# A one-core fp32 block pair kernel: the second in-projection as five Strassen pairs, with its inputs, trig tables and residual copies placed around the pooling blocks

## The reference

```python
h = x @ w_in                       # 1024 x 2368
x_q, x_kv, k_rope_raw, gate_a, u_pool, gate_b = jnp.split(h, splits, axis=-1)   # 512 256 64 512 512 512
y_a = mla_branch(x_q, x_kv, k_rope_raw, positions, ...) * jax.nn.silu(gate_a)
y_b = pool_branch(u_pool, pool_w, pool_scale) * jax.nn.silu(gate_b)   # window means of 2, 4, 8, 16, minus u; one 128x128 product per group
x = layer_norm(alpha * x + concatenate([y_a, y_b]) @ w_out, ln_g, ln_b)
```

## Time and profile before

| | us |
|---|---|
| median of 3 runs (lowest, highest) | 1684.1 (1683.61, 1685.53) |
| the profiled execution's own time | 1683.6 |
| its span, first to last instruction | 1681.8 |
| PE busy in the span | 1666.5 |
| mean granted TensorE clock | 0.997 |

### The profile page before, as it was taken

One profiled execution on the slowest core, in us unless ns is written; L12 is line 12 of the kernel. 1 busy time (PEld: TensorE's weight loads), 2 busy tenths in 40 slices (PEclk: granted clock), 3 DMA queues, 4 the chain that ended last, 5 costly groups with the idle time before them and its releaser, 6 DMA issues.

```text
span 1681.8 us, 20879 instructions
## 1 busy us (share of the span) xinstructions
PE 1666.5 (99%) x7597; PEld 1373.9 (82%) x7597; DVE 1256.2 (75%) x1494; ACT 795.6 (47%) x1066; POOL 452.0 (27%) x270
## 2 busy tenths in 40 slices
PE   9999999999999999999999999999999999999998
PEld 7788788888787888888888888888888888788786
DVE  6478791369999888888888879889737936777654
ACT  5667741236854433444344444455332327566531
POOL 4223222100015654555454000005432442201000
PEclk9999999999999999999999999999999999999999
DMA  7111112053412232222322974762322221010351
GB/s 265 52 48 37 50 51 76 25 213 94 169 51 88 76 98 75 75 87 84 91 75 96 327 267 153 247 195 62 101 88 63 88 88 31 26 63 26 114 218 75
DMA packets 161098, 176.99 MB, mean 105 GB/s; under 512 B 13566, under 2 KB 114692, under 8 KB 161028
## 3 DMA queue, kind: packets, MB, share of 16 engines
q1 hardware_dynamic: 158708, 167.67, 30.7%
q10 hardware_dynamic: 2320, 8.39, 1.3%
HBM read 140.38 MB, written 35.65 MB: 105 GB/s over the span
## 4 chain that ended last, share of the span: by engine, by line
PE 93%; DVE 4%; ACT 1%; issue 1%; DMA 1%; DVEq 0%; SPq 0%; ACTq 0%
PE ps L962 31%; PE ps L2603 27%; PE ps L2557 19%; PE ps L2849 5%; PE ps L2834 3%; PE ps L2499 1%; PE ps L2685 1%; PE ps L2888 1%; PE ps L2806 1%; DVE pt_lo L2376 1%; PE ps L2523 1%; DVE prob L2333 1%; PE ps L2822 1%; DMA x_tok<-in_x 1%; ACT pt_hi L1646 0%
## 5 line engine op out<-in xcount | busy, mean ns | idle before, releaser
L985 POOL TENSOR_TENSOR w_lo<-w_raw,w_hi 128x1024 fp32r<-128x1024 f32 x52 | 138.0, 2654 | 594.1 <-ACT w_hi L1097 592.3
L2603 PE MATMUL ps<-hop_hi_P,wop_hi_P 128*128 128x512 f32 x672 | 263.6, 392 | 2.0 <-DVE u L1974 0.8
L2603 PE MATMUL ps<-hop_lo_P,wop_hi_P 128*128 128x512 f32 x672 | 262.9, 391 | 0.0
L2603 PE MATMUL ps<-hop_hi_P,wop_lo_P 128*128 128x512 f32 x672 | 262.8, 391 | 0.0
L991 POOL TENSOR_TENSOR wop_lo_P<-pair_sum,wop_hi_P 128x512 fp32r<-128x512 f32 x90 | 137.3, 1526 | 351.5 <-ACT wop_hi_P L1108 351.5
L962 PE MATMUL ps<-h_hi,w_hi 128*128 128x512 f32 x688 | 214.1, 392 | 0.0
L962 PE MATMUL ps<-h_lo,w_hi 128*128 128x512 f32 x688 | 211.9, 389 | 0.0
L962 PE MATMUL ps<-h_hi,w_lo 128*128 128x512 f32 x688 | 211.8, 389 | 0.0
L962 PEld LDWEIGHTS ps<-h_hi,w_hi 128*128 128x128 f32 x688 | 128.2, 188 | 30.0 <-issue 4.3
L2603 PEld LDWEIGHTS ps<-hop_hi_P,wop_hi_P 128*128 128x128 f32 x672 | 126.9, 189 | 30.5 <-DVE u L1974 1.6
L962 PEld LDWEIGHTS ps<-h_lo,w_hi 128*128 128x128 f32 x688 | 129.1, 188 | 27.1
(11 more groups left out here) (386 smaller groups left out, 3403.8 us busy)
## 6 DMA issues: line engine op xcount, KB each, us to landing
pair_raw<-in_w_up SPq DMA_DIRECT2D x48, 512.0 KB, 4.9
w_raw<-in_w_in SPq DMA_DIRECT2D x46, 512.0 KB, 3.9
dn_raw<-gu_park SPq DMA_DIRECT2D x84, 256.0 KB, 3.9
dn_raw<-in_w_down SPq DMA_DIRECT2D x60, 256.0 KB, 3.1
gu_park<-up_cv SPq DMA_DIRECT2D x24, 512.0 KB, 2.6
out_raw<-in_w_out SPq DMA_DIRECT2D x30, 256.0 KB, 2.8
x_tok<-in_x SPq DMA_DIRECT2D x4, 1024.0 KB, 8.1
x_park<-xs SPq DMA_DIRECT2D x1, 4096.0 KB, 13.2
```

What stands on the lines that cost most here:

```text
L985: nc.gpsimd.tensor_tensor(lo[:, :], raw[:, :], hi[:, :].bitcast(f32), ALU.subtract).then_inc(w_lo_done, 1)
L2603: mm = nc.tensor.matmul(dst, w[q][:, k, :], x[q][:, k, :], start=a, stop=b, skip_group_check=True)
```

## The change

Of the 19 blocks only the 8 for pooling and the rope key stay blocks, and they come first (the head blocks are now u and gate_b of group 0). The 10 others (6 latents, 4 gates) become five Strassen pairs after them: kv; q 0 and 1; q 2 and 3; gates 0 and 1; gates 2 and 3. The PE stream and what it waits for:

```diff
-            for i in range(2, Q_TILES + KV_TILES):
...
-            pe.wait_ge(ga_done, 3)
-            project(N_KR, 0, ps[0], h_hi, h_lo)
+            block_with(N_POOL + 2, ps[0], lambda: (pe.wait_ge(final_gain, 16), pe.wait_ge(gb_done, 1), by_token(0)))
+            by_token(1)
+            pe.wait_ge(rstd3_spread, 1)
+            block_with(N_POOL + 3, ps[1], lambda: (by_token(2), pool_product(0)))
+            by_token(3)
...
+            block_with(N_KR, ps[0], lambda: pool_product(3))
...
+        IN_RUN = ("P1", "P6", "P5", "P2", "P7")
+        IN_ORDER = [(q, 0) for q in IN_RUN]
+        for n in range(IN_PAIRS - 1):
+            IN_ORDER += [("P1", n + 1), ("P4", n), ("P3", n)] + [(q, n + 1) for q in IN_RUN[1:]]
+        IN_ORDER += [("P4", IN_PAIRS - 1), ("P3", IN_PAIRS - 1)]
...
+                if q == "P1":
+                    pe.wait_ge(*((yb_done, 4), (kr_scaled, 1), (lat_done, 2), (lat_done, 4), (lat_done, 6))[n])
+                elif q == "P6":
+                    pe.wait_ge(*((tok_copied, NT), (gb_done, 4), (lat_done, 1), (lat_done, 3), (lat_done, 5))[n])
+                    if n in (2, 4):
+                        pe.wait_ge(root2_done, n // 2)
+                elif q == "P2":
+                    pe.wait_ge(s1c_done, PAIRS + n + 1)
+                else:
+                    need = {"P7": "U2", "P4": "U3", "P3": "C22"}.get(q)
+                    if need:
+                        pe.wait_ge(sums_done, in_sums(need, n))
+                pe.wait_ge(wop_lo_done, in_made(q, n))
...
+            for q, n in IN_ORDER:
+                in_product(q, n)
+                if (q, n) == ("P1", 2):
+                    pe.wait_ge(acc_kv_done, KV_TILES)
+                    spread_mean_squares(acc_kv, 0)
+                elif (q, n) == ("P2", 3):
+                    pe.wait_ge(acc_q_done, Q_TILES)
+                    pe.wait_ge(lat_done, Q_TILES + KV_TILES)
+                    spread_mean_squares(acc_q, 1)
...
                 if j == 0:
+                    pe.wait_ge(ga_done, 1)
+                elif j == 1:
                     pe.wait_ge(ga_done, 4)
...
+                elif j == 3:
+                    pe.wait_ge(ga_done, 2)
```

The order of the pairs (n = 0 to 4), first on DVE, then on ACT:

```diff
+            for n in range(IN_PAIRS):
+                in_third_sums(n)
+                if n == 2:
+                    latent_factor(0, T2)
+                elif n == 3:
+                    latent_factor(1, T1)
+                    latent_factor(1, T2)
+                    latent_normed(0)
+                    latent_normed(1)
+                elif n == 4:
+                    latent_low(2)
+                    gate2(1)
+                    gate2(0)
+                in_result(n, 1)
+                if n == 4:
+                    gate2(3)
+                in_result(n, 0)
+                if n + 1 < IN_PAIRS:
+                    in_second_sum(n + 1)
+                if n == 1:
+                    latent_factor(0, T1)
+                elif n == 2:
+                    latent_normed(4)
+                    latent_normed(5)
+                elif n == 3:
+                    latent_normed(2)
+                    latent_normed(3)
+                    latent_low(0)
+                if n + 2 < IN_PAIRS:
+                    in_weight_sums(n + 2)
+            gate2(2)
...
+            for n in range(-1, IN_PAIRS):
+                last = n + 1 == IN_PAIRS
+                if not last:
+                    in_high("P7", n + 1)
+                    in_first_sum(n + 1)
+                if n == 1:
+                    latent_root(0)
+                if not last:
+                    in_high("P4", n + 1)
+                if n == 3:
+                    latent_high(0)
+                    latent_high(1)
+                if 0 <= n < 3:
+                    latent_square(PAIR_LATS[n][1])
+                elif n >= 3:
+                    gate_tanh2(2 * n - 5)
+                if not last:
+                    in_high("P3", n + 1)
+                if n == 4:
+                    park_gate(3)
+                if 0 <= n < 3:
+                    latent_square(PAIR_LATS[n][0])
+                elif n >= 3:
+                    gate_tanh2(2 * n - 6)
+                for q in IN_NEXT:
+                    if n + 2 < IN_PAIRS:
+                        in_high(q, n + 2)
+                if n == 2:
+                    latent_root(1)
+                if n == 3:
+                    latent_high(2)
+                    latent_high(3)
+                    act.wait_ge(wop_lo_done, in_made("P3", IN_PAIRS - 1))
+                    high(N_UQ)
+                    park_gate(1)
+                    park_gate(0)
+                elif n == 4:
+                    park_gate(2)
+            act.wait_ge(product, in_run("P5", IN_PAIRS - 1))
+            act.wait_ge(latn_done, Q_TILES + KV_TILES)
+            high(N_UQ + 1)
+            act.wait_ge(pos_in, POS_BACK)
+            act.wait_ge(sums_done, in_sums("C12", IN_PAIRS - 1))
+            swap_halves(0, kr_raw)
```

The weights of a pair have one buffer, loaded in two halves on SP:

```diff
+            for n in range(IN_PAIRS):
+                if n == 0:
+                    sp.wait_ge(block_done, N_KR)
+                for f in range(2):
+                    if n >= 1:
+                        sp.wait_ge(pair_sum_done, 4 * PAIRS + 4 * n)
+                        sp.wait_ge(wop_lo_done, in_made(("P2", "P4")[f], n - 1))
+                    sp.dma_start(in_raw[f][:, :, :], w2_v[:, :, IN_COLS[n][f]:IN_COLS[n][f] + P]).then_inc(pair_in[f], 16)
+            sp.wait_ge(wop_lo_done, in_made("P3", IN_PAIRS - 1))
+            sp.wait_ge(product, in_run("P5", IN_PAIRS - 1))
 ...
```

More of the change, by code:

```diff
@@ L846, in _, with nope_load @@
             load(n, 0, *[(dst[:, :, h, :], uq[:, :, h, NOPE:QK]) for h in range(HEADS)])
-            for b in range(2):
+            def nope_load(b):
                 n = N_UQ + 1 + b
@@ L1066, in _ @@
+            pool.wait_ge(gate_parked[1], GATE + 16)
+            low(N_UQ + 1)
+            low(N_UQ + 2)
+            latent_low(5)
+            for n in range(N_UQ + 3, N_BLOCKS):
+                low(n)
             pool.wait_ge(block_done, N_BLOCKS - 1)
@@ L1535, in _ @@
[L1535 to L1549 removed]
+                act.dma_start(res_park[t], tok_out[t % 2][:, :]).then_inc(res_parked[t % 2], 16)
@@ L1576, in _, with park_pooled @@
-            gate(0)
-            park_pooled(3)
-            gate(1)
-            gate(2)
-            gate(3)
-            for q in range(2):
-                act.wait_ge(gate_parked[q], GATE + 16 * HEADS // 2)
+                    act.wait_ge(y_parked, 16 * (g - 1))
+                nc.scalar.activation(y_pool[:, g % 2, :], ps[3 if g == 0 else 1][:, :], ACT.Tanh, scale=0.5).then_inc(th_done, 1)
+            def park_pooled(g):
+                act.wait_ge(yb_done, g + 1)
+                act.dma_start(y_park[4 + g], y_pool[:, g % 2, :]).then_inc(y_parked, 16)
@@ new lines, in _ @@
+            pooled_gate(1)
+            pool_gate(2, "P6")
+            mix_sum("P4")
+            mix_low("P7")
+            mix_low("P6")
+            pooled(3)
+            pool_weight(3)
+            pooled_gate(2)
+            pool_gate(3)
+            in_weight_sums(0)
+            pooled_gate(3)
+            mix_low("P4")
+            for parked in res_parked:
+                dve.wait_ge(parked, 16 * NT // 2)
+            dve.wait_ge(block_done, read(N_KR))
+            V.tensor_tensor(kr_out[:, :], ps[0][:, :], rstd3[:, :], ALU.mult).then_inc(kr_scaled, 1)
@@ L2723, in _, with pool_product, block_with @@
-            pe.wait_ge(lat_done, 5)
-            project(N_POOL, 0, ps[0], h_hi, h_lo)
+            def pool_product(g):
+                pe.wait_ge(pl_lo, g + 1)
+                pe.wait_ge(pw_hi_done, 2 * g + 2)
+                if g >= 1:
+                    pe.wait_ge(yb_done, g)
+                else:
+                    pe.wait_ge(u_done, 1)
+                matmul3(pe, ps[2], pw_hi[:, :], pw_lo[:, :], pooled_hi, pooled_lo, True, True).then_inc(pool_mm, 1)
+            def block_with(n, dst, middle):
+                pe.wait_ge(w_lo_done, n + 1)
+                wh, wl = blocked(n)
+                for k in range(8):
+                    mm = matmul3(pe, dst, wh[:, k, :], wl[:, k, :], h_hi[:, k, :], h_lo[:, k, :], k == 0, k == 7)
+                    if k == 7:
+                        mm.then_inc(block_done, 1)
+                    elif k == 3:
+                        middle()
```

645 lines of the change are left out of this document (433 added, 212 removed).

## The result

The changed kernel takes 1688.62 us (median of 8, 1686.78 to 1689.79), the kernel before 1683.69 in the same comparison (median of 8). The ratio is 1.0028, 95% interval 1.0018 to 1.0039: slower by some 5 us, where 1682.9 and no change had been forecast. The profiled execution of after took 1689.35 itself, its span is 1687.2.

The account below looks back on a forecast made before the run. PE was taken as the bound, busy 1666.5 of 1681.8 us. Matmuls removed, start, tail and clock gave 1683.6 - 13.7 + 0.9 + 10.5 + 1.6 = 1682.9 us, range 1677.0 to 1687.3.

Parts of the forecast that it names:

- PE is relieved of 13.7 us.: Matmuls on PE: ten blocks (109.1 us) go and five pairs (95.4 us) come, 13.7 us less.
- PE waits 0.9: Start of the stage, by_token(0): PE waits 0.9 us for DVE's product behind tanh; bounds 0 and 2.
- P7 waits 0.7: Pair five: P7 waits 0.7 us for U2, behind a second root ending at 3.1.
- 2.1: Pair five: PE waits 2.1 us at P4 for U3, 0.9 if DVE were free.
- rival 3: Pairs one to three: POOL becomes the bound through collisions with DVE, 1688.0 us; chance 0.12.
- That is 7.7 in all from j=0 to j=6: Up-projection: PE waits 2.9 us at j=1, about 1.0 at j=5 and 3.8 at j=6.
- 25.5 before, now 26.4: Rope chain, first four swaps' end to j=6's first low part: 25.5 us before, plus 0.9 for POOL holding DVE.
- about 1 us for a collision: Price of one lock wait between DVE and POOL, taken as about 1 us from POOL's 2.28 less 1.30.
- tanh 34.1, last gate 35.4: Tail, counted from P7 of pair four's end: ACT's tanh done at 34.1 us, DVE's last gate at 35.4.
- I add 1.6: Granted clock: one drop to 0.50 behind j=6 costs 1.6 us; bounds 0 and 3.2.
- Nothing changes: Behind j=6: all runs as before, no cost besides the clock's.
- Rival 2: Waits mostly hidden, only U3's 0.9 and 2 us at j=1 and j=6 remaining: 1673.0 us; chance 0.05.

Follow-up runs that it names:

- e2: The changed kernel with gate 2 in a tile of its own, so tanh(2) needn't wait until gate 0 is parked; 1685.04 us.
- e1: The changed kernel with its new DRAM buffers allocated behind y_park instead of ahead of it; 1687.58 us.
- e4: The changed kernel with 30 matmuls that compute nothing put into PE's gaps, ahead of the wait at j=1 and at j=5; 1686.07 us.
- e7b: As e7, with the POOL order of e6, and DVE's low part of latent 0 moved behind U3 and C22 of pair five; 1682.41 us.
- e8: As e7, but the key read back behind P5 into a free tile, gates parked behind tanh(2), gate 1 in its own place; 1678.80 us.
- e10: As e9, with the parked key's read put ahead of SP's wait for the pairs' last low part; 1676.94 us.
- e3: The changed kernel with the two PSUM pairs of pair five exchanged, so j=1 needs the third gate, not the last; 1688.11 us.
- e7: As e5, with the key's swaps in their own tile ahead of the last two tanh, second weights' high part ahead of the last; 1682.91 us.
- e6: The changed kernel with POOL's low part of the kv latent put behind that of the next weights; 1689.00 us.
- e5: As e2, and DVE makes C12 and its scaling ahead of gate 3's product; 1684.76 us.
- e9: As e8, with high and low parts of the first two plain queries put between the rotations on ACT and DVE; 1678.57 us.

## Why the prediction was wrong, point by point

- **"PE is relieved of 13.7 us."** Nearly. From the head blocks' end to j=0 PE's stretch went from 200.9 to 190.2 us; without after's waits of 0.6 and 1.5 that is 12.8 less, and 0.9 us of the forecast isn't found.
- **"PE waits 0.9"** at the start: 0.6. **"P7 waits 0.7"**: no wait; the second root ended 1.1 us behind P7 of pair four, where I had 3.1. **"2.1"** at P4: 1.5; of the 2.0 us of the early root 1.3 went again, as the two latents behind it took 4.1 us on DVE against the 2.8 I had. Pairs one to four: no wait, so rival 3, the one that had the right sign, is wrong in its place and its mechanism; that its 1688.0 lies near the measured time is luck.
- **The step that failed is the tail behind pair five: "That is 7.7 in all from j=0 to j=6".** It was 11.5. The mechanism was the right one: j=1 waited for DVE's last gate (4.0, forecast 2.9), j=6 for the first low part. The terms were mis-sized. The last gate came 35.8 us after the end of P7 of pair four (1345.0) against 35.4, j=0 at 26.1 against 27.2, and "25.5 before, now 26.4" for the rope chain was 28.4: first swaps' end at 1386.7, low part at 1415.1. I had charged the chain one lock wait of 0.9 for a new POOL operation; it met 4.1 us of them against 1.4 before, and where I had taken "about 1 us for a collision" they cost 1.0, 0.9 and 2.2. Together 0.4 + 1.1 + 2.0 is 3.5 of the 3.8 us; starts are read to a tenth.
- I also walked tanh(2) past the wait for its tile: "tanh 34.1, last gate 35.4" has no parked gate in it. The scaled input was there at 31.8, 1.2 us before my 33.0, and the wait took that back: tanh(2) began 1.7 us after it. e2 gives this wait's price, 1.8 us from j=0 to j=6.
- **"I add 1.6"** for the clock: 2.7. One drop behind j=6 counted, as forecast, but it lasted 6.8 us and the one in the earlier trace rows that priced it 3.4.
- **"Nothing changes"** behind j=6: 1.9 us in the profiled execution, at loads of the output projection. It comes and goes between executions (e1, e2, e4 none; e7b 1.8).
- The sum again, against the own times: 0.9 (relief) less 1.6 (start, P7, P4) plus 3.8 (tail) plus 1.1 (clock) plus 1.9 (end) plus 0.3 (time outside the span, 2.1 instead of 1.8) is 6.4; 1682.9 became 1689.35. The range failed with it: every upper bound was for one term, and the tail and the clock came near theirs together while a wait outside the change was added.
- **Rival 2 ("mostly hidden", 1673.0)** was set aside because "program order on ACT speaks against". That was right of the change as made. e8 to e10 show what another order of ACT, DVE and SP, with tiles moved, gives: 1678.8 down to 1676.9. The 1673.0 wasn't reached, and what the last 4 us would need isn't shown.

## What to carry to other kernels

When a stage is shortened by matmuls alone, the chain of the other engines that ends it can become the bound, as here: walk that chain from its first fixed event, and price every wait by what it does to the chain, not by its own length. A wait that is removed without shortening the chain only moves (e3); one operation taken out of the chain can bring in a late DMA instead (e7). Fix the order first, and see when reloads land beside the loads issued with them.

## What the runs showed of the hardware that I had not expected

- Two lock waits on DVE moved when POOL's order was changed and didn't shrink (operations of 2.19 and 3.40 us in after, two others of 3.43 and 3.41 in e6).
- In the up-projection the drops of the granted clock to 0.50 had two lengths: 3.4 us at waits of 2.0 to 2.8 us (e7b, e2, e4, e3; the drop of the earlier trace rows, behind no wait, had the same), 6.8 us at waits of 3.2 to 5.8 (after, e1, e2, e3, e5, e6, e7). In 5.9 us of a drop PE did 14 matmuls of 512 columns where 26 fit at the full clock (after, 1380.86 to 1386.76).
- The length of a wait alone didn't decide: at 2.3 us in e2 the clock fell, at 2.7 us in e8 it didn't. PE in stretches, e2 around the end of its wait at 1380.74, then e8 behind its wait that ended at 1374.22:

```profile
1380.00:1384.00 4.00, 3.26 (x10) 2.53 (x11) 0.68 (x1) 2.74 (x3) 1.60 (x1) 0.71 0.65 257
```

```profile
1374.00:1378.00 4.00, 3.78 (x17) 3.16 (x18) 1.67 (x2) 3.93 (x5) 0.00 (x0) 1.00 1.05 213
```

- A key of half a megabyte, issued at 1367.4 ahead of eight table loads, was usable at 1373.9 in e7; the same read issued at 1364.1 in e9 held up the weights behind it instead: their high part came 5.8 us after their first issue, against 4.2 in e10, where the key was read 5.5 us earlier, and 4.1 in after. SP's queue took about 0.5 us to issue each of these (eight table loads in 3.7 us in after).
